# Routing stage: four last key lists taken beside the one-hots, and who makes which one-hot

## What is computed

```python
s1 = jnp.einsum('nhd,kd->nhk', q[:, :, 0], k_sub1)      # 8 heads, 128 keys
s2 = jnp.einsum('nhd,kd->nhk', q[:, :, 1], k_sub2)
v1, i1 = lax.top_k(s1, PEER_TOPK)                        # 16 best of 128
v2, i2 = lax.top_k(s2, PEER_TOPK)
cand = (v1[..., :, None] + v2[..., None, :]).reshape(N, PEER_HEADS, 256)
cidx = (i1[..., :, None] * PEER_NKEYS + i2[..., None, :]).reshape(N, PEER_HEADS, 256)
sc, pos = lax.top_k(cand, PEER_TOPK)
idx = jnp.take_along_axis(cidx, pos, axis=-1)
wts = jax.nn.softmax(sc, axis=-1)
...
act = jax.nn.gelu(einsum('nhed,nd->nhe', u_exp[ib], xb))
out = einsum('nhe,nhed->nd', wb * act, v_exp[ib])
```

## Time and profile before

| | us |
|---|---|
| median of 3 runs | 5611.01 |
| lowest, highest | 5606.44, 5633.81 |
| the profiled execution | 5617.95 |
| its span | 5616.4 |
| TensorE busy in the span | 5031.6 (90%) |
| VectorE busy | 3409.6 (61%) |
| ScalarE busy | 1724.3 (31%) |
| GpSimd busy | 1379.4 (25%) |

### The profile page before, as it was taken

The page is one execution under the profiler, slowest core; times in us unless marked ns, Lnnn a source line. Parts: engine busy times, 40 slices in busy tenths (PEclk is TensorE's granted clock), DMA queues, the critical chain, the costliest instruction groups (busy, mean ns, idle before and its releaser), DMA issues. The chain is left out here.

```text
span 5616.4 us, 61825 instructions
## 1 busy us (share of the span) xinstructions
PE 5031.6 (90%) x23397; PEld 4101.4 (73%) x23397; DVE 3409.6 (61%) x4459; ACT 1724.3 (31%) x2274; POOL 1379.4 (25%) x1059
## 2 busy tenths in 40 slices
PE   8979999999997888989794589999999999988994
PEld 3347888888885645868683579998899899866773
DVE  7742211115674243322558968888878788878888
ACT  6843112122222111121423623333333332223332
POOL 0300000000100122000004824333333334444443
PEclk9989999999998899989897889999999999999997
DMA  9842323233322455432511699999999999999997
GB/s 361 310 153 94 105 96 101 84 103 102 118 98 94 147 193 192 162 101 101 167 38 31 143 347 383 380 371 378 364 381 373 375 382 375 389 388 399 405 405 318
DMA packets 460055, 1334.66 MB, mean 238 GB/s; under 512 B 135868, under 2 KB 193084, under 8 KB 377198
## 3 DMA queue, kind: packets, MB, share of 16 engines
q1 hardware_dynamic: 336180, 667.06, 33.6%
q0 software_dynamic: 96576, 623.69, 28.3%
q10 hardware_dynamic: 27072, 40.91, 2.1%
HBM read 1206.06 MB, written 126.56 MB: 237 GB/s over the span
## 5 line engine op out<-in xcount | busy, mean ns | idle before, releaser
L229 PE MATMUL ps<-w_hi,act_hi 128*128 128x512 f32 x3040 | 1198.0, 394 | 48.7 <-DVE act_lo L1036 23.0
L231 PE MATMUL ps<-w_hi,act_lo 128*128 128x512 f32 x3040 | 1188.8, 391 | 0.0
L230 PE MATMUL ps<-w_lo,act_hi 128*128 128x512 f32 x3040 | 1188.8, 391 | 0.0
L224 DVE TENSOR_TENSOR w_lo<-w_stage,w_hi 128x2048 fp32r<-128x2048 f32 x152 | 348.1, 2291 | 1151.4 <-ACT w_hi L220 1148.9
L2405 ACT ACTIVATE x_hi<-x_stage 128x1024 fp32r<-128x1024 f32 x512 | 543.4, 1061 | 1508.5 <-DMA x_stage<-u_turned 746.3
L2485 DVE TENSOR_TENSOR x_lo<-x_stage,x_hi 128x1024 fp32r<-128x1024 f32 x512 | 625.3, 1222 | 373.6 <-ACT x_hi L2405 372.6
L2332 POOL DMA_INDIRECT u_ring<-u_exp,idx_all x256 | 598.2, 2337 | 852.2 <-DVE u_ring L2503 807.2
L2359 PE MATMUL ps<-act_hi,x_hi 128*128 128x384 f32 x2048 | 695.2, 339 | 68.4 <-DVE x_lo L2485 65.9
L229 PEld LDWEIGHTS ps<-w_hi,act_hi 128*128 128x128 f32 x3040 | 574.9, 189 | 172.5 <-issue 44.0
L2359 PE MATMUL ps<-x_hi,cx_hi 128*128 128x512 f32 x1536 | 612.2, 399 | 95.9 <-DVE cx_lo L2496 80.5
L2361 PE MATMUL ps<-act_hi,x_lo 128*128 128x384 f32 x2048 | 690.8, 337 | 0.0
(11 more groups left out here) (306 smaller groups left out, 5613.5 us busy)
## 6 DMA issues: line engine op xcount, KB each, us to landing
x_stage<-u_turned SPq DMA_DIRECT2D x256, 512.0 KB, 8.7
x_stage<-v_exp SPq DMA_DIRECT2D x256, 512.0 KB, 9.0
w_stage<-w_ada SPq DMA_DIRECT2D x96, 1024.0 KB, 6.4
w_stage<-w_in SPq DMA_DIRECT2D x96, 1024.0 KB, 5.2
d_w<-w_buf SPq DMA_DIRECT2D x6, 4096.0 KB, 20.7
gwr<-d_w SPq DMA_DIRECT2D x128, 192.0 KB, 10.8
d_gw<-gob ACTq DMA_DIRECT2D x128, 192.0 KB, 6.6
gwr<-d_gw SPq DMA_DIRECT2D x128, 192.0 KB, 10.3
```

Source lines behind the costliest of these rows:

```text
L224: dve.tensor_tensor(w_lo[:, q % 2], w_in_st[:, q], w_hi[:, q % 2].bitcast(F32), ALU.subtract).then_inc(w_split, 1)
L229: pe.matmul(out, lhs[0], rhs[0], start=first, stop=False)
L230: pe.matmul(out, lhs[0], rhs[1], start=False, stop=False)
L231: return pe.matmul(out, lhs[1], rhs[0], start=False, stop=last)
```

## The change

1. **Lists.** The middle stage takes only the list n = 15 at its end. The lists 16 to 19, of tiles 1 to 4, are taken in the routing stage at the start of VectorE's part for each of these tiles, with the same `top16`. The scores stay where they were; they get a name of their own (`mid_sc`), and the routing stage leaves their room free.
2. **One-hots.** All first one-hots are VectorE's (16 a tile, one 1024-wide comparison each). Of the 16 second ones of a tile ScalarE makes eight, GpSimd seven and VectorE the last. ScalarE's weighted one-hot is Relu(weight - weight x distance), eight operations 128 wide with scale and bias per partition, for which the negated weights are kept as a fourth row of `id_t`.
3. **Ids.** TensorE turns the ids of tile t + 1 behind sixteenth 13 of tile t, and ScalarE copies them there.
4. **Spacing.** `settle` issues one sixteenth's one-hots where it issued two, and the later `extra()` calls two where they issued one. ScalarE makes its one-hot two sixteenths ahead of the copies.

The diff, cut to its core:

```diff
-                for t in range(TT):
-                    lists((n_ch - 1) * TT + t)
+                lists((n_ch - 1) * TT)
+        return sc, sc_at
...
+    late_head = 2 * PH - 4
+    late_n = (D // NCOL - 1) * TT
...
+    TURN_AT = NQ - 3
...
-    FIRST_BY = 4 * ("act", "dve", "act", "pool")
-    SECOND_BY = 4 * ("dve", "pool", "dve", "dve")
+    SECOND_BY = 7 * ("act", "pool") + ("act", "dve")
...
+        def first_hot(dve, Q):
             if Q >= RING1:
-                eng.wait_ge(w_ready, 2 * (Q - RING1) + 2)
+                dve.wait_ge(w_ready, 2 * (Q - RING1) + 2)
...
+            turn_ids(0)
             for t in range(ND):
-                turn_ids(t)
                 for q in range(NQ):
                     spread(t, q)
+                    if q == TURN_AT and t < ND - 1:
+                        turn_ids(t + 1)
...
+            def ids(t):
+                act.wait_ge(id_ready, t + 1)
+                act.activation(id_t[:, t % 2, 3], ps[:, 5, 2 * P:3 * P], ACT.Copy, scale=-1.0)
+                act.activation(id_t[:, t % 2, 0:3].rearrange("p a n -> p (a n)"), ps[:, 5, 0:3 * P],
+                               ACT.Copy).then_inc(id_taken, 1)
...
                 act.wait_ge(s_dist, 8 * made)
-                if Q >= RING1:
-                    act.wait_ge(w_ready, 2 * (Q - RING1) + 2)
-                act.activation(one1[:, Q % RING1], dist[:], ACT.Relu, scale=-1.0, bias=1.0).then_inc(s_one1["act"], 1)
+                if Q >= RING2:
+                    act.wait_ge(w_ready, 2 * (Q - RING2) + 2)
+                for j in range(8):
+                    n = 8 * q + j
+                    made_ = act.activation(one2[:, Q % RING2, j], dist[:, j], ACT.Relu, scale=id_t[:, t % 2, 3, n:n + 1],
+                                           bias=id_t[:, t % 2, 2, n:n + 1])
+                made_.then_inc(s_one2["act"], 1)
...
                 for q in range(NQ):
-                    near(t, q)
-                    if q > 0:
-                        take(t, 2 * q - 2)
-                        take(t, 2 * q - 1)
-                    if q == 10:
+                    if q + 2 < NQ:
+                        near(t, q + 2)
+                    take(t, 2 * q)
+                    take(t, 2 * q + 1)
+                    if q == 9:
                         weights(t + 1)
-                take(t, NW - 2)
-                take(t, NW - 1)
+                    if q == TURN_AT and t < ND - 1:
+                        ids(t + 1)
...
             for t in range(TT):
                 equal = iter(range((t - 1) * NQ, t * NQ) if 0 < t <= ND else ())
+                if t > 0:
+                    slot = (late_n + t) % 4
+                    top16(4, lambda j: late_sc[:, slot, j], lambda j: top_all[:, t, late_head + j],
+                          lambda j: topi_all[t][:, late_head + j], first_hots=0)
```

More of the change, by code:

```diff
@@ L1514, in mid_stage @@
             ob = nc.alloc_sbuf_tensor_at("mid_ob", [P, TT, NCOL], F32, offset=room)
+            x2_at = -(-nc.sbuf_base // 32) * 32
             x2 = sb(st, "mid_x2", [P, TT, D])
@@ L1906, in _ @@
                         lists(n + 4)
-                for t in range(TT):
-                    lists((n_ch - 1) * TT + t)
+                lists((n_ch - 1) * TT)
+        return sc, sc_at
     n_ch = D // NCOL
     project_stage("yo", a["w_gla_o"], d_m, c_o0, g_o0, gated=True, credit=True, then=a["w_out"], loaded=True)
-    mid_stage(c_o0 + n_ch, g_o0 + n_ch, c_o0 + 2 * n_ch, g_o0 + 2 * n_ch, t_groups)
+    late = mid_stage(c_o0 + n_ch, g_o0 + n_ch, c_o0 + 2 * n_ch, g_o0 + 2 * n_ch, t_groups)
     main_scope.close()
@@ L1918, in _build @@
     lk = link(None, "dve")
-    route(nc, a, stage, sem, sb, kc, ps, (idx_all, wt_all, top_all, topi_all), area, d_w, lk)
+    route(nc, a, stage, sem, sb, kc, ps, (idx_all, wt_all, top_all, topi_all, late), area, d_w, lk)
     experts(nc, a, stage, sem, sb, ps, (idx_all, wt_all), act_hi, act_lo, area, d_post, d_w, d_gw, d_f3, d_x2, d_h2)
 def route(nc, a, stage, sem, sb, kc, ps, route_sb, area, d_w, lk):
-    idx_all, wt_all, top_all, topi_all = route_sb
+    idx_all, wt_all, top_all, topi_all, (late_sc, late_at) = route_sb
+    late_head = 2 * PH - 4
+    late_n = (D // NCOL - 1) * TT
     ident = kc[:, K_ID:K_ID + P]
@@ L1932, in route, with maker @@
     RING1, RING2 = 4, 5
+    TURN_AT = NQ - 3
     half = 4 * TT * KD * P
     spare = 4 * ND * KD * P
-    FIRST_BY = 4 * ("act", "dve", "act", "pool")
-    SECOND_BY = 4 * ("dve", "pool", "dve", "dve")
-    def makers(table, Q):
-        who = table[Q % len(table)]
-        return who, sum(table[n % len(table)] == who for n in range(Q + 1))
+    SECOND_BY = 7 * ("act", "pool") + ("act", "dve")
+    def maker(Q):
+        who = SECOND_BY[Q % NQ]
+        return who, sum(SECOND_BY[n % NQ] == who for n in range(Q + 1))
     at_sb = nc.alloc_sbuf_tensor_at
@@ L2028, in spread @@
                 Q = t * NQ + q
-                who, made = makers(FIRST_BY, Q)
-                pe.wait_ge(s_one1[who], made)
-                who, made = makers(SECOND_BY, Q)
+                pe.wait_ge(s_one1, Q + 1)
+                who, made = maker(Q)
                 pe.wait_ge(s_one2[who], made)
@@ L2059, in near @@
                 if made > 1:
-                    act.wait_ge(s_one1["act"], made - 1)
+                    act.wait_ge(s_one2["act"], made - 1)
                 for j in range(8):
@@ L2079, in _ @@
             weights(0)
+            ids(0)
             for t in range(ND):
-                act.wait_ge(id_ready, t + 1)
-                act.activation(id_t[:, t % 2].rearrange("p a n -> p (a n)"), ps[:, 5, 0:3 * P], ACT.Copy).then_inc(id_taken, 1)
                 act.wait_ge(id_taken, t + 1)
+                near(t, 0)
                 for q in range(NQ):
-                    near(t, q)
-                    if q > 0:
-                        take(t, 2 * q - 2)
-                        take(t, 2 * q - 1)
-                    if q == 10:
+                    if q + 2 < NQ:
[3 more added lines that the diff above has]
+                    if q == 9:
                         weights(t + 1)
-                take(t, NW - 2)
-                take(t, NW - 1)
+                    if q == TURN_AT and t < ND - 1:
+                        ids(t + 1)
             weights(TT - 1)
@@ L2107, in extra, with settle, top16 @@
                         dve.wait_ge(id_taken, t + 1)
-                    if makers(FIRST_BY, Q)[0] == "dve":
-                        first_hot(dve, "dve", Q)
-                    if makers(SECOND_BY, Q)[0] == "dve":
+                    first_hot(dve, Q)
+                    if maker(Q)[0] == "dve":
                         second_hot(dve, "dve", Q)
-            def settle():
-                extra(2)
+            def settle(hots):
+                extra(hots)
                 lk.sync()
                 dve.sem_inc(gate, 1)
-            def top16(n, values, best, where):
+            def top16(n, values, best, where, first_hots=1):
                 for r in range(2):
                     eight = slice(8 * r, 8 * r + 8)
-                    settle()
+                    hots = 1 if r else first_hots
+                    settle(hots)
                     for j in range(n):
                         lk.mark(dve.max(best(j)[:, eight], values(j)))
-                    settle()
+                    settle(hots)
                     for j in range(n):
@@ L2178, in _ @@
                 lk.mark(dve.tensor_reduce(sel[:, t, 0], hot[:], AX.X, ALU.add))
-                extra()
+                extra(2)
                 lk.sync()
```

40 lines of the change are left out of this document (18 added, 22 removed).

## The result

| | before | after |
|---|---|---|
| median of 11 runs | 5619.64 us (5606.44 to 5633.81) | 5653.89 us (5646.42 to 5665.33) |
| profiled execution (span) | 5617.95 us (5616.4) | 5650.52 us (5649.0) |
| routing stage alone, from its first instruction to its last weights | 238.7 us | 299.3 us |
| one-hot phase, from tile 0's ids to the last copy | 186 us | 247.5 us |

The ratio is 1.0062, between 1.0052 and 1.0072 at 95%: the change costs about 35 us (29 to 40). I had forecast no difference, 5611 us, and a range that ended at 5630.

A forecast was written before the change was run, and what follows sets the result against it. GpSimd and its turnover between tiles were taken to bound a period, VectorE hardly faster. Terms -21.7 + 5.9 + 22 - 6 = +0.2 us on the median of 5611.01 gave 5611 us, range -15 to +15 (chance 0.68).

The forecast's parts named there:

- (1): Start of the routing stage: four lists leave the middle stage, so routing starts earlier, -21.7 us; tile 4's path pays +5.9.
- (2): VectorE in a one-hot period: its load falls from 59 to 54.2 us.
- (3): ScalarE in the one-hots: a pair of sixteenths goes from 6.70 to 8.15 us (6.8 to 9.6), 66.3 us a tile.
- my own sum by ScalarE: One-hot phase if ScalarE sets it: 24 pairs of 8.15 us plus 2.5 and 2, 200 us.
- (4): GpSimd in a tile: 44.2 us of second one-hots plus 25.6 of stops by VectorE's tensor-tensors, 69.8 us.
- My sum by GpSimd: One-hot phase if GpSimd sets it: 209 us plus 6 for the last three products, 215 us.
- (5): Border between tiles: despite ids turned early, GpSimd still waits some 4.5 us; gain on the bound nothing.
- (6): One-hot phase, first ids to last copy: 186 us becomes 208, the middle of 200 and 215, +22.
- the 75 that I had named as a sign of being wrong: Spacing of tiles' ids: some 67 to 70 us expected; 56, or 75 and more, would show the forecast wrong.
- (7): End of the routing stage: VectorE leaves the one-hots about 10 us ahead of the last copy, not 4, -6 us.
- The case on the slow side: Rival in the one-hot phase: GpSimd stopped for tensor-tensors' full length, turnover on top; +32 us, 5643 us, chance 0.08.
- The case of a short ramp: Rival on ScalarE: eight ramps take near 1.06 us, GpSimd bounds; about -13 us, 5598 us, chance 0.14.

## Why the prediction was wrong, step by step

**(1) The lists: right.** Forecast -21.7, measured -21.9 (routing starts 19.6 us earlier, and that execution's middle stage ran 2.3 us late: the list that began at 2968.35 began at 2970.62). Tile 4's part is 33.9 us; I had 34.

**(2) VectorE's load: right.** Busy 54.05 and 52.0 us in the first two periods, forecast 54.2. Its wait for products is 67.9 us in all, where I had 30 to 45.

**(3) ScalarE's load: the step that failed.** Forecast 8.15 us for a pair, measured 10.56. Two errors in one term. The ramp: I took 2.44 for eight pieces, measured 3.19. I chose the distances as the nearest row, but they carry one operand per partition and the ramp two; each adds 0.09 us (293 ns with none, 389 with one, 478 with two). With it the one-hot takes 5.56 us, not 4.88: 0.68 us a pair, 16 us in 24 pairs. The Trainium skill (ScalarE: Activation LUTs, "What ACT_TABLE_LOAD costs") puts an activation with immediates at 186 ns + 0.833 ns an element, each per-partition operand at about 93 more, and the overlap of neighbours at about 93. An estimate from these figures for 128 elements is 293, 386 and 479 ns, and the traces agree within 3 ns.

The second error is larger: I carried the 3.27 us of copies and waits over from before as a constant. But 1.12 of it were waits for products made at 2.4 GHz, by a TensorE that stood 2.77 us at a time. They became 2.86 once TensorE stood 3.9 us and came back at 1.2 GHz: 1.73 us a pair, 42 us in 24. Added to my own sum by ScalarE (200 us), the two errors give 258; the phase was 247.5, since not every pair is as long as the one shown (in the first two tiles a pair comes every 10.14 us, 162.3 / 16, and 24 of those are 243, with 4 us at the end). I had the clock column in front of me, 0.89 to 0.84, and never asked what a longer absence of ScalarE would do to it.

The Trainium skill (TensorE: Matmul & The Clock Gate, "A second HAM failure mode: psum-queue depth-cycling") describes another kernel of this kind, whose TensorE pauses between groups while it cycles through PSUM banks and whose clock goes to and fro between its two levels. The traces agree: 1.00 with 3.93 us a group before, 0.66 with 6.4 after. It belonged among the rivals.

**(4) GpSimd's load: too high, and not the bound.** Forecast 69.8 a tile; measured 64.3 in the changed kernel and 66.6 with four banks, where it worked without a break. That a stop costs less than the full length of VectorE's operation was right; the price was 3.2 us a tile too high. My sum by GpSimd came near the phase with four banks (215 and 217.0) because I also took off 3 us a tile for stops that fall into GpSimd's waits, and the first of those waits, 4.86 us, has no tensor-tensor but one that begins 0.06 us before its end. Two errors cancelled.

**(5) The turnover: off, through (3).** GpSimd stands 15.9 us at a border, not 4.5: it waits for the ids, which TensorE turns behind product 13, and the products are behind. With four banks it stands 4.86.

**(6) The phase: wrong, through (3).** Forecast 208 us (+22), measured 247.5 (+61.5). The ids came 80 and 82 us apart, beyond the 75 that I had named as a sign of being wrong.

**(7) The end: right.** VectorE leaves the one-hots 11.6 us ahead of the last copy; I had 10. It gives back 7.4 us. (The landing of the last half, 3214 + 20.7, was 3234.7 and not 3235.5; nothing hangs on it.)

The sum with the measured terms: -21.9 + 5.9 + 61.5 - 7.4 = +38, against +35 (29 to 40) by the ratio. Between the two profiled executions it is +32.6: there the routing stage ended 41.0 us later (the 38, the 2.3 us by which the middle stage was late, and 0.7 for the second copy of tile 0's ids, which stands ahead of the phase), and what follows it was 8.4 us shorter, within the spread named above.

**The rivals.** The case on the slow side gave 5643 us, the nearest to the result, by a mechanism that four banks rule out as the bound here: with it fully at work the kernel took 5626 us. It was the right size by accident. The case of a short ramp had the right eye for the term, and its sign wrong. The range failed twice. Its end for ScalarE's pair (9.6) was set by the ramp alone, and lay under the 10.56 measured. And that end wasn't carried through: 24 x 9.6 + 4.5 is a phase of 235 us, where the range stopped at 215, and would have given about +27 us, 5638.

**What stays open.** The clock and ScalarE's absence can't be separated fully, since none of these edits sets the clock by itself. The nearest is the pair of groups in the thirteen-matmul run, and it prices the clock at a microsecond of a pair; the split ramp changes both. What makes the clock fall ahead of one group and not ahead of another isn't shown. Why the second period of the version with the old one-hots shared out anew is 68.3 us with no engine busy for 60 of it wasn't found.

## What to carry to other kernels

Where two engines pass work through two banks, the time that one of them is away is more than a cost to be added to its own load: it sets how long the other stands, and can set with what clock that one comes back, and so the waits of the first. Of a pair's time carried over from a profile, take apart what is work and what is wait before it is called constant, and cut the longest absence first (more banks, or the work in two pieces around a copy), before work is shared out anew. And take the price of an operation from a row with the same kinds of operands, not only the same size.

## What the runs showed of the hardware

- TensorE after the same standstill of 2.00 us did a group of 32 records in 3.93 us in one place and in 5.44 in the next (thirteen idle matmuls): a standstill's length alone doesn't tell the clock of what follows.
- Ahead of groups of 32 records TensorE stood 2.52 us and began at a clock of 0.50, and stood 3.48 us and began at 0.99, in the same trace (the split ramp).
- A hold of ScalarE longer by 0.64 us, in 24 pairs, lengthened the stage by 19 us (238.7 to 257.7), while the clock over the groups shown of tile 0 went from 1.00 to 0.73.
- ScalarE's 128-wide activation lasts 293 ns with immediates, 389 with one operand per partition and 478 with two; in a row of eight they begin 0.20, 0.29 and 0.39 us apart.
- The stop of GpSimd by VectorE's tensor-tensors adds up to less than their length: with four banks 31.4 us of them in a tile cost it 22.4 us. Their length less some 0.4 us for each group gave 56.9 us for a period of before (measured 57.6), and 69.8 for one with four banks (measured 66.6), which is too much.
